# A decoder step on one Trainium2 core: the last 16 prompt queries as two leading chunks of the sample pipeline, and prompt output rows turned behind the next scores

## The chip, the cores and the metric

The program runs on one NeuronCore of a Trainium2 chip. The core has a matrix engine (PE, with its weight loads shown as PEld), a vector engine (DVE), a scalar engine (ACT), a general engine (POOL), and SP, which here only issues DMAs. The metric is the device time in microseconds of one execution; lower is better. PE works on operands in SBUF and writes to PSUM; DVE and ACT move results from PSUM to SBUF. The engines run their own instruction lists and wait for each other on semaphores.

## The reference

One inference step over 1024 prompt tokens (with 16 learned tokens ahead of them, so 1040 rows) and 8 sample tokens, each of which has a paged past of 4096 tokens. A first layer is a gated linear recurrence, the second is latent attention: all heads share a latent key/value row of 256 numbers and a rotary key of 64.

```python
def mla_scores(q_lat, q_rope, ckv, krope):
    s = jnp.einsum('bqhr,bkr->bhqk', q_lat, ckv) + jnp.einsum('bqhp,bkp->bhqk', q_rope, krope)
    return s.astype(jnp.float32) * ATTN_SCALE
...
    s = jnp.where((k_pos[None, :] <= q_pos[:, None])[None, None], s, MASK_VALUE)
    p = jax.nn.softmax(s, axis=-1).astype(ckv.dtype)
    return jnp.einsum('bhqk,bkr->bqhr', p, ckv)
```

The sample tokens do the same over `cache_ckv[page_table]` and `cache_krope[page_table]` (4096 rows each) and their own new row. After attention come an output projection, a squared-ReLU MLP and a final norm.

## The kernel before, in words

All 1048 tokens are held as columns of one array `h` (1050 wide). The stages run one after the other, each a block of instruction lists for the five engines with a barrier between blocks: load, recurrence, projection, MLP, `latents`, `query_latent`, `prompt_attention`, `sample_attention`, projection, MLP, `finish`. Two of them matter here.

**`prompt_attention`** covers prompt queries 0 to 1023: 8 heads times 8 tiles of 128 queries are 64 units, in an order written out by hand (`ORDER_ROWS`). For each unit s PE turns the probabilities of s (`turn_probs`, L1647, transposes into the two banks of `M`), computes the scores of s + 2 (`scores`, L1635 and L1638), does pieces of projection work for the next head (`piece`, L185), and multiplies by the values of s (`values`, L1665). After every fourth unit the four finished rows of output tiles are turned as well (`turn_out_rows`, L1655), in a bank of `M` that the turned probabilities also use. ACT copies turned probabilities out of `M` (L1731), copies the turned output rows (L1740) and does the exponentials (L1721); it also splits rotary queries (L1714).

**`sample_attention`** handles the rest: the 16 last prompt queries (the "tail": 8 heads times 16 queries fill 128 rows) and the 8 sample tokens. First PE turns the key projection (L2084) and forms the latent queries (L2099). Then, before, the tail is done by itself: the 1040 prompt keys, read back from the output by SP (L2015, L2016), are turned (L2090, L2092, L2105), copied, scored in four blocks of 260 (L2113, L2114), the row maxima, exponentials and turned probabilities follow (L2272, L2053, L2126), and the values (L2132). In the same place the sample tokens' scores with each other's new rows are formed (`cross`, L2119, L2120). Only then the pipeline over the paged past starts: for each of 8 tokens two chunks of 16 key tiles. A chunk is four spans of four tiles: `turn(u)` transposes the keys of a span (L2145) and for every second span the rotary keys (L2153), ACT copies even spans (L2033), DVE odd ones (L2295) and the rotary keys (L2301). One turn of the loop for chunk n is: first turn of chunk n + 1, values of n - 1 (L2185), scores of n (L2165, L2170), three more turns, turned probabilities of n (L2177). The four spans' scores stand in four groups of 32 rows. POOL gathers the pages (L2007, L2008) into a ring of four; the ring's last slot holds the prompt keys until the tail is done. A closing part (L2212 to L2235) joins the chunks and applies the value projection `w_uv`.

The 16 chunk loops, the queue order on SP and POOL and the order on each engine are all written out in the code; no scheduler moves anything.

Of the kernel before, what the change touches and what calls it, by code (L numbers as in the profile page):

```python
# [6 lines left out]
F32 = mybir.dt.float32  # L7
# [65 lines left out]
def setup(nc, ctx, dram):  # L73
# [11 lines left out]
    k.w_raw = sb("w_raw", [P, 2, WB])  # L85
    k.w_hi = sb("w_hi", [P, 2, WB], F32R)
    k.w_lo = sb("w_lo", [P, 2, WB], F32R)
    k.rstd = sb("rstd", [P, T])
# [31 lines left out]
    k.ckv_one = sb("ckv_one", [P, KC, DEC])  # L120
    k.kr_one = sb("kr_one", [ROPE, DEC])
# [1057 lines left out]
def latents(k, keys):  # L1179
# [5 lines left out]
    with ExitStack() as mem:  # L1185
# [13 lines left out]
        with nc.Block() as block:  # L1199
# [83 lines left out]
            def _(dve):  # L1283
# [24 lines left out]
                nc.vector.tensor_copy(k.kr_one[:, :], kr32[:, PROMPT:NTOK]).then_inc(k.g_free, 1)  # L1308
# [9 lines left out]
                link(nc.vector.tensor_copy(k.ckv_one[:, :, :], c32[:, :, PROMPT:NTOK]))  # L1318
# [126 lines left out]
def prompt_attention(k, keys, scratch):  # L1445
# [52 lines left out]
    with ExitStack() as mem:  # L1498
# [42 lines left out]
        with nc.Block() as block:  # L1541
# [45 lines left out]
            def _(pe):  # L1587
# [309 lines left out]
PAIR_COLS = SPAN * P  # L1897


def sample_attention(k, scratch):  # L1900

    nc, dr = k.nc, k.dram
    every = DEC * CHUNKS
    with ExitStack() as mem:
        def sb(name, shape, dt=F32):
# [6 lines left out]
        uk_turned = sb("uk_turned", [P, HEADS * KC, P])  # L1914
        w_kv = k.w_raw[:, :, :].rearrange("p a n -> p (a n)").rearrange("p (t h n) -> p t h n", t=KC, n=P)
        q_all = k.rstd[:, 0:DEC * (KC + 2) * LANE].rearrange("p (b t n) -> p b t n", b=DEC, n=LANE)
# [13 lines left out]
        o_lat = uk_turned[:, :, :].rearrange("p a n -> p (a n)")[:, 0:KC * HEADS * ONE].rearrange(  # L1930
            "p (t h n) -> p t h n", t=KC, n=ONE)
        o_one = sb("o_one", [P, HEADS, T - SEQ])

        c_rows = pages[:, RING - 1, 0:NT * KV].rearrange("p (t n) -> p t n", n=KV)
        kr_rows = ropes[:, RING - 1, 0:NT * ROPE].rearrange("p (t n) -> p t n", n=ROPE)
        keys_out = o_all[:, :, :].rearrange("p a n -> p (a n)")
        c_turned = keys_out[:, 0:KC * PROMPT].rearrange("p (t n) -> p t n", n=PROMPT)
        kr_turned = keys_out[0:ROPE, KC * PROMPT:(KC + 1) * PROMPT]
        tail_prob = pages[:, RING - 1, NT * KV:NT * KV + PROMPT]
# [38 lines left out]
        def tile_of(n, j):  # L1978
            return pages[:, n % RING, j * KV:(j + 1) * KV]
# [14 lines left out]
        with nc.Block() as block:  # L1994
            @block.gpsimd
            def _(pool):
# [526 lines left out]
```

## Time and profile before

| | |
|---|---|
| median of 3 runs | 3271.95 us (3263.16 to 3274.47) |
| profiled execution, its own time | 3266.1 us |
| its span in the trace | 3264.3 us |
| PE busy | 2927.2 us, 90% of the span |
| mean granted clock of PE | 0.942 of full speed |
| start of the sample stage's first instruction on PE | 2102.49 us |

The span runs from the first to the last instruction of the profiled execution; the stages follow each other in it. Positions in the trace (such as 2102.49) are microseconds from its start. A wait is shown with what ended it, as `[13.79 <-DMA late<-in_causal]`. The granted clock is 1.00 at 2.4 GHz and 0.50 at 1.2 GHz.

### The profile page before, as it was taken

The numbers are of one execution on the slowest core, as the hardware profiler recorded it, in microseconds if no ns is written. First come the engines' busy times: TensorE is split into PE (matmuls) and PEld (weight loads), VectorE is DVE, ScalarE is ACT, GpSimd is POOL, SyncE is SP. The second block draws the span as 40 slices with busy tenths as digits, with TensorE's granted clock in tenths as the row PEclk, the third lists the DMA queues.
The fourth block names the chain that finished last, engine by engine and source line by source line (L and its number), as shares of the span: only waits on it lengthen the run. The fifth ranks groups of instructions, "written<-read, shape, count | busy, mean of one in ns | idle before, by whom it ended". The sixth has DMA issues, their size and how long they took to land. (4 is left out here: it accounts for less than half of the span.)

```text
span 3264.3 us, 51288 instructions
## 1 busy us (share of the span) xinstructions
PE 2927.2 (90%) x21729; PEld 2772.6 (85%) x21729; DVE 1371.4 (42%) x1689; ACT 527.5 (16%) x810; POOL 785.3 (24%) x455
## 2 busy tenths in 40 slices
PE   6999899749899999999866889699788999999998
PEld 6888888749899999999755888566588999999997
DVE  6466666641633333222545555334315333222333
ACT  3222222120200000000222333323102000000001
POOL 2112211012333333333211100001033333333331
PEclk9999999859999999999878999879799999999999
DMA  3111111020111111111110000246221111111112
GB/s 100 47 46 46 48 56 46 21 93 26 52 46 46 45 46 46 46 46 46 37 30 25 26 28 32 100 161 265 77 62 39 46 46 46 46 46 46 46 46 72
DMA packets 213553, 185.32 MB, mean 57 GB/s; under 512 B 22720, under 2 KB 201200, under 8 KB 211344
## 3 DMA queue, kind: packets, MB, share of 16 engines
q1 hardware_dynamic: 174544, 116.19, 11.8%
q0 software_dynamic: 4608, 41.95, 3.3%
q10 hardware_dynamic: 34240, 24.75, 2.5%
q8 instruction: 136, 2.23, 0.3%
q14 instruction: 25, 0.20, 0.0%
HBM read 163.97 MB, written 18.89 MB: 56 GB/s over the span
## 5 line engine op out<-in xcount | busy, mean ns | idle before, releaser
L157 POOL CAST w_hi<-w_raw 128x1024 fp32r<-128x1024 f32 (+3 forms) x206 | 210.1, 1020 | 2165.3 <-PEq L960 1530.7
L185 PE MATMUL G<-xg_lo_a,w_hi 128*128 128x350 f32 (+1 forms) x1980 | 464.3, 338 | 115.8 <-POOL w_lo L159 58.8
L159 POOL TENSOR_TENSOR w_lo<-w_raw,w_hi 128x1024 fp32r<-128x1024 f32 (+3 forms) x206 | 541.9, 2630 | 16.5
L185 PEld LDWEIGHTS G<-xg_lo_a,w_hi 128*128 128x128 f32 (+1 forms) x1980 | 343.2, 194 | 135.1 <-issue 61.9
L185 PE MATMUL G<-xg_hi_a,w_lo 128*128 128x350 f32 (+1 forms) x1980 | 449.8, 330 | 0.0
L185 PE MATMUL G<-xg_hi_a,w_hi 128*128 128x350 f32 (+1 forms) x1980 | 448.6, 330 | 0.0
L1123 DVE TENSOR_TENSOR h<-h,G 128x1050 f32<-128x1050 f32 x128 | 159.7, 1248 | 520.6 <-PE G L185 520.6
L185 PEld LDWEIGHTS G<-xg_hi_a,w_hi 128*128 128x128 f32 (+1 forms) x1980 | 350.4, 194 | 0.6
L185 PEld LDWEIGHTS G<-xg_hi_a,w_lo 128*128 128x128 f32 (+1 forms) x1980 | 348.7, 194 | 0.6
L185 PE MATMUL G<-a_hi,w_hi 128*128 128x350 f32 x1536 | 332.1, 324 | 0.0
L185 PE MATMUL G<-a_lo,w_hi 128*128 128x350 f32 x1536 | 332.1, 324 | 0.0
L185 PE MATMUL G<-a_hi,w_lo 128*128 128x350 f32 x1536 | 329.8, 322 | 0.0
L1065 ACT ACTIVATE a_hi<-ua 128x1050 fp32r<-128x1050 f32 x64 | 69.4, 1085 | 1222.4 <-DVE ua L1113 1222.4
L185 PEld LDWEIGHTS G<-a_lo,w_hi 128*128 128x128 f32 x1536 | 263.4, 189 | 0.0
L185 PEld LDWEIGHTS G<-a_hi,w_hi 128*128 128x128 f32 x1536 | 261.6, 189 | 0.0
L185 PEld LDWEIGHTS G<-a_hi,w_lo 128*128 128x128 f32 x1536 | 261.5, 189 | 0.0
L1110 DVE TENSOR_TENSOR ua<-G,rstd 128x1050 f32<-128x1050 f32 x64 | 80.1, 1252 | 403.8 <-PE G L185 403.7
L185 PE MATMUL G<-xg_lo_b,w_hi 128*128 128x350 f32 x960 | 209.2, 326 | 39.8 <-POOL w_lo L159 34.6
L185 PE MATMUL G<-xg_hi_b,w_lo 128*128 128x350 f32 x960 | 208.8, 326 | 0.0
L185 PE MATMUL G<-xg_hi_b,w_hi 128*128 128x350 f32 x960 | 208.2, 325 | 0.0
L185 PEld LDWEIGHTS G<-xg_lo_b,w_hi 128*128 128x128 f32 x960 | 164.6, 191 | 42.4 <-POOL w_lo L159 35.0
L1116 DVE TENSOR_TENSOR a_lo<-ua,a_hi 128x1050 fp32r<-128x1050 f32 x64 | 140.2, 2191 | 73.7 <-ACT a_hi L1065 73.7
(349 smaller groups left out, 3386.9 us busy)
## 6 DMA issues: line engine op xcount, KB each, us to landing
w_raw<-in_w_up SPq DMA_DIRECT2D x64, 512.0 KB, 4.1
w_raw<-in_w_down SPq DMA_DIRECT2D x64, 512.0 KB, 3.4
o_scratch<-o_head SPq DMA_DIRECT2D x8, 525.0 KB, 5.3
o_in<-o_scratch ACTq DMA_DIRECT2D x4, 1050.0 KB, 9.3
o_in<-a_scratch ACTq DMA_DIRECT2D x4, 1050.0 KB, 9.2
w_raw<-in_hg_wq SPq DMA_DIRECT2D x8, 512.0 KB, 4.3
w_raw<-in_hg_wf SPq DMA_DIRECT2D x8, 512.0 KB, 4.2
w_raw<-in_hg_wi SPq DMA_DIRECT2D x8, 512.0 KB, 4.2
```

Source lines behind the costliest of these rows:

```text
L157: nc.gpsimd.tensor_copy(high, raw).then_inc(k.w_hi_done, 1)
L159: nc.gpsimd.tensor_tensor(low, raw, high, ALU.subtract).then_inc(k.w_split, 1)
L185: last = nc.tensor.matmul(out, w(a, t), x(b, t, c), start=(t == 0 and (a, b) == ORDER[0]), stop=(t == nk - 1 and (a, b) == ORDER[-1]))
L1065: nc.scalar.activation(a_hi[:, half, j, :], a, ACT.Copy).then_inc(a_hi_there, 1)
L1110: nc.vector.tensor_tensor(in3(u), tile(k, (g0 + 1 + j) % 2), in3(k.rstd[:, :]), ALU.mult).then_inc(k.g_free, 1)
L1116: nc.vector.tensor_tensor(a_lo[:, half, j, :], a, a_hi[:, half, j, :], ALU.subtract).then_inc(a_ready, 1)
L1123: nc.vector.tensor_tensor(h, h, tile(k, (g0 + 1 + t) % 2), ALU.add).then_inc(k.g_free, 1)
```

## The change

Two edits. The first is in `prompt_attention`: `turn_out_rows` stands behind `scores(s + 2)` instead of ahead of it, at the 15 units where it occurs inside the loop.

The second is in `sample_attention`. The separate computation for the tail is gone. Its first 1024 keys become two chunks at the head of the pipeline (`EARLY` = 2, of one span each instead of four, with all 128 rows of the tail in place of four groups of 32), so there are 18 steps and spans 0 and 1 belong to the tail. The tail's last 16 keys (its own) are scored beside `cross` and have a softmax part of their own; the three parts are joined on DVE during later chunk loops (`tail_rests`, `tail_join`) with one exponential on ACT. `late`, the mask for the own keys, no longer belongs to what `rows_in` counts. POOL waits for the prompt rows before the first gather. `w_uv` has a buffer of its own and is loaded by SP behind the prompt rows, not by ACT. `uk_turned`, `tail_q` and others live in the space of `w_hi` and `w_lo`, and `ckv_one` and `kr_one` hold 24 columns instead of 8.

```diff
                     turn_probs(s)
+                    if s + 2 < UNITS:
+                        scores(s + 2)
                     if s % 4 == 0 and s:
                         turn_out_rows(s // 4 - 1)
-                    if s + 2 < UNITS:
-                        scores(s + 2)
...
+EARLY = SEQ // (SPAN * P)
+def spans_of(n):
+    return [n] if n < EARLY else [EARLY + (n - EARLY) * GROUPS_1 + j for j in range(GROUPS_1)]
+def chunk_of(u):
+    return u if u < EARLY else EARLY + (u - EARLY) // GROUPS_1
...
             def _(pool):
                 nc.gpsimd.memset(q_all, 0.0).then_inc(cleared, 1)
+                nc.gpsimd.memset(tail_qr, 0.0).then_inc(cleared, 1)
...
+                pool.wait_ge(rows_in, 64)
                 for n in range(every):
                     if n == RING - 1:
+                        pool.wait_ge(valued, EARLY)
                         pool.wait_ge(tail_valued, 1)
                     if n >= RING:
-                        pool.wait_ge(valued, n - RING + 1)
+                        pool.wait_ge(valued, EARLY + n - RING + 1)
...
             def _(sp):
+                for h in range(HEADS):
+                    sp.dma_start(late[h * TAIL:(h + 1) * TAIL, :], dr["causal"][0:TAIL, 0:TAIL]).then_inc(late_in, 16)
                 sp.dma_start(own[:, :], dr["ckv_sample"][:, 0, :]).then_inc(own_in, 16)
-                for h in range(HEADS):
-                    sp.dma_start(late[h * TAIL:(h + 1) * TAIL, :], dr["causal"][0:TAIL, 0:TAIL]).then_inc(rows_in, 16)
+                sp.wait_ge(rows_in, 64)
+                sp.dma_start(w_uv[:, :, :, :], dr["w_uv"].rearrange("(t p) h n -> p t h n", p=P)).then_inc(uv_in, 16)
...
+                pe.wait_ge(rows_in, 64)
+                turn(0)
+                pe.wait_ge(ql_out, KC + 2)
+                pe.wait_ge(tail_q_out, 3)
...
+                turn(1)
+                scores(0)
+                pe.wait_ge(own_out, 2)
+                pe.wait_ge(tail_exped, 1)
+                pe.transpose(T_BANK[0:TAIL, 0:P], tail_prob, k.ident[:, :]).then_inc(tail_pt_done, 1)
+                pe.wait_ge(tail_pt_out, 1)
+                nc.tensor.matmul(O[:, 1, :], tail_pt, c_rows[0:TAIL, FULL, :], start=True, stop=True).then_inc(tail_valued, 1)
+                turn_probs(0)
+                for n in range(1, steps):
+                    later = spans_of(n + 1) if n + 1 < steps else []
+                    if n == EARLY - 1:
                         values(n - 1)
+                        scores(n)
+                        for u in later:
+                            turn(u)
+                    else:
+                        for u in later[:1]:
+                            turn(u)
+                        values(n - 1)
+                        scores(n)
+                        if n == EARLY + 3:
+                            pe.wait_ge(tail_summed, 1)
...
+                def tail_join():
+                    dve.wait_ge(tail_weighed, 1)
+                    link(nc.vector.tensor_tensor(tail_sums[:, :], tail_sums[:, :], tail_weight[:, :], ALU.mult))
+                    link(nc.vector.reduce_sum(tail_stat[:, 2:3], tail_sums[:, :], AX.X))
+                    link(nc.vector.reciprocal(tail_stat[:, 3:4], tail_stat[:, 2:3]))
+                    link(nc.vector.tensor_scalar(tail_weight[:, :], tail_weight[:, :], tail_stat[:, 3:4], None, ALU.mult))
+                    link(nc.vector.tensor_scalar(o_tail[:, 0, :], o_tail[:, 0, :], tail_weight[:, 0:1], None, ALU.mult))
+                    for a in range(1, parts):
+                        link(nc.vector.scalar_tensor_tensor(out=o_tail[:, 0, :], in0=o_tail[:, a, :],
+                                                            scalar=tail_weight[:, a:a + 1], in1=o_tail[:, 0, :],
+                                                            op0=ALU.mult, op1=ALU.add))
+                    dve.sem_inc(tail_summed, 1)
```

PE in `prompt_attention`, unit 28, before: the turned probabilities (L1647), the output rows (L1655), then the scores of unit 30 (L1635, L1638).

```order
L1647 MATMUL M<-ident,prob 128x128 x3
L1655 MATMUL M<-ident,a_o_rows 128x128 [waits a_turn_out,a_o_there]
L1655 MATMUL M<-ident,a_o_rows 128x128 x3
L1635 MATMUL G<-xg_lo_a,xg_hi_a 128x512 [waits a_exp]
L1635 MATMUL G<-xg_hi_a,xg_lo_a 128x512
```

The same place in the changed kernel, whose line numbers are 3 higher here: the end of the scores of unit 30, the output rows, and the first product of the next piece (L188).

```order
L1638 MATMUL G<-xg_hi_a 128x384
L1641 MATMUL G<-kr_lo,xg_lo_a 128x384
L1641 MATMUL G<-kr_hi,xg_lo_a 128x384
L1658 MATMUL M<-ident,a_o_rows 128x128 [waits a_turn_out,a_o_there]
L1658 MATMUL M<-ident,a_o_rows 128x128 x3
L188 MATMUL G<-xg_lo_a,w_hi 128x350 [waits a_piece_out]
```

The four transposes and their wait stand behind ten score products instead of ahead of them.

PE at the head of the sample stage, before: from the latent queries (L2099) to the tail's values (L2132), twelve of its rows in their order.

```order
L2099 MATMUL M<-q_one,uk_turned 128x24 x15
L2105 MATMUL G<-ident,pages 128x128 x16
L2113 MATMUL G<-o_all,one_pt 128x260 [waits s_tail_out,s_tail_q_out]
L2113 MATMUL G<-o_all,one_pt 128x260
L2114 MATMUL G<-o_all,one_pt 128x260
...
L2119 MATMUL M<-rstd,ckv_one 8x64 [waits s_ql_out]
L2119 MATMUL M<-rstd,ckv_one 8x64
L2120 MATMUL M<-rstd,kr_one 8x64
L2126 MATMUL G<-ident,pages 128x128 [waits s_tail_exp]
L2126 MATMUL G<-ident,pages 128x128 x7
L2126 MATMUL M<-ident,pages 16x128
L2132 MATMUL M<-pages,keys_turned 128x256 [waits s_own_out,s_tail_pt_out]
```

The changed kernel from the same queries (L2115) to the scores of the second early chunk (L2154; `spare_lo` holds the tail's queries and its own keys' probabilities).

```order
L2115 MATMUL M<-q_one,spare_hi 128x24 x15
L2130 MATMUL G<-ident,pages 128x128 [waits s_rows_in]
L2130 MATMUL G<-ident,pages 128x128 x7
...
L2190 MATMUL M<-ckv_one,spare_lo 128x16 x2
L2191 MATMUL M<-kr_one,spare_lo 128x16
L2130 MATMUL G<-ident,pages 128x128 x8
L2154 MATMUL M<-keys_turned,spare_lo 128x512 [waits s_pair_out,s_span_out0]
L2154 MATMUL M<-keys_turned,spare_lo 128x512
L2160 MATMUL M<-ropes_turned,spare_lo 128x2x128 x2
L2197 MATMUL M<-ident,spare_lo 16x128 [waits s_tail_exped,s_own_out]
L2199 MATMUL G<-pages,spare_lo 128x256 [waits s_tail_pt_out]
L2167 MATMUL M<-ident,one_prob 128x128 [waits s_pt_out,s_exped]
```

The queries no longer stand behind the wait for the rows, and the tail's keys are turned, scored and used with the pipeline's instructions.

DVE in chunk step 4 of the changed kernel: the maxima (L2295, L2296), the join of the tail's parts (L2328 to L2334), and only then the copy of the next odd span (L2284), which before stood right behind the maxima.

```order
L2296 TENSOR_SCALAR one_bottom<-one_tops 128x1 [waits dve_chain]
L2328 TENSOR_TENSOR tail_sums<-tail_sums,tail_weight 128x3 [waits s_tail_weighed]
L2329 TENSOR_REDUCE tail_stat<-tail_sums 128x1 [waits dve_chain]
L2330 RECIPROCAL tail_stat<-tail_stat 128x1 [waits dve_chain]
L2331 TENSOR_SCALAR tail_weight<-tail_weight,tail_stat 128x3 [waits dve_chain]
L2332 TENSOR_SCALAR spare_lo<-spare_lo,tail_weight 128x256 [waits dve_chain]
L2334 SCALAR_TENSOR_TENSOR spare_lo<-spare_lo,tail_weight 128x256 [waits dve_chain] x2
L2284 COPY keys_turned<-G 128x1024 [waits dve_chain,s_scored,s_span_done]
```

Seven instructions stand between the maxima and the copy in that step; two stand there in step 3, one in step 5.

## Rows read from the trace of the kernel before

**Rows 1.** The page: engine busy time, then the granted PE clock in 40 slices.
```profile
PE 2927.2 (90%) x21729; PEld 2772.6 (85%) x21729; DVE 1371.4 (42%) x1689; ACT 527.5 (16%) x810; POOL 785.3 (24%) x455
...
PEclk9999999859999999999878999879799999999999
```

**Rows 2.** Windows: stretch, its length, busy PE, PEld, DVE, ACT, POOL, clock, DMA.
```profile
1790.00:2080.00 290.00, 258.96 (x1682) 232.97 (x1680) 153.90 (x388) 108.68 (x242) 22.70 (x32) 0.98 0.08 26
2102.00:2165.00 63.00, 43.16 (x174) 32.94 (x175) 10.90 (x32) 6.82 (x8) 8.71 (x10) 0.58 0.47 180
2165.00:2323.00 158.00, 151.86 (x1694) 104.44 (x1692) 77.29 (x111) 51.41 (x78) 22.47 (x24) 0.99 0.55 211
```

**Rows 3.** Timeline, sample stage: start, length, engine, line, instruction, idle before.
```profile
2102.49 3.65 PE L2084 MATMUL G<-ident,w_raw 128*128 128x128 f32 x16 [3.22 <-PEq L1541]
...
2106.17 1.22 DVE L2251 COPY uk_turned<-G 128x1024 f32<-128x1024 f32 x1 [2.13 <-PE G L2084]
...
2119.93 1.92 PE L2090 MATMUL G<-ident,ropes 128*64 128x128 f32 x8 [13.79 <-DMA late<-in_causal]
...
2122.15 7.02 PE L2099 MATMUL M<-q_one,uk_turned 128*128 128x24 f32 x32
...
2128.99 3.20 PE L2105 MATMUL G<-ident,pages 128*128 128x128 f32 x16
...
2152.84 7.32 PE L2132 MATMUL M<-pages,keys_turned 128*128 128x256 f32 x18 [1.04 <-DVE keys_turned L2283]
```

**Rows 4.** Timeline, PE in the chunk loops.
```profile
2173.03 1.04 PE L2145 MATMUL G<-ident,pages 128*128 128x128 f32 x8
...
2182.89 1.04 PE L2145 MATMUL G<-ident,pages 128*128 128x128 f32 x8
...
2184.30 1.93 PE L2185 MATMUL G<-pages,one_pt 128*32 128x256 f32 x32
2186.05 1.90 PE L2165 MATMUL M<-keys_turned,rstd 128*32 128x512 f32 x16
...
2188.74 1.97 PE L2145 MATMUL G<-ident,pages 128*128 128x128 f32 x16
...
2191.38 1.09 PE L2145 MATMUL G<-ident,pages 128*128 128x128 f32 x8 [0.24 <-DVE keys_turned L2295]
```

**Rows 5.** DMA view, 2102:2108: queue, packets, MB, share; then 2100:2325, landing us.
```profile
q1 hardware_dynamic: 1947, 1.29, 73.3%
...
pages<-in_cache_ckv,page_rows POOLq DMA_INDIRECT x16, 8.3
```

**Rows 6.** Timeline, DVE and ACT instructions of a chunk.
```profile
2169.38 0.69 DVE L2306 TENSOR_REDUCE one_tops<-M 128x1 f32<-128x512 f32 x1 [2.17 <-PE M L2170]
2170.11 0.15 DVE L2307 TENSOR_SCALAR one_bottom<-one_tops 128x1 f32<-128x1 f32 x1
...
2173.23 0.60 ACT L2046 ACTIVATE one_pt<-M 128x512 f32<-128x512 f32 x1 [0.95 <-PE M L2177]
```

**Rows 7.** Windows: clock under thin work, at the stage's end, and in it.
```profile
2330.00:2352.00 22.00, 21.48 (x98) 21.12 (x98) 0.39 (x2) 0.00 (x0) 0.00 (x0) 0.50 0.00 1
...
2132.00:2135.00 3.00, 0.89 (x5) 0.67 (x4) 1.23 (x1) 1.93 (x2) 0.00 (x0) 1.00 0.00 0
2135.00:2136.00 1.00, 1.00 (x3) 0.38 (x3) 0.00 (x0) 0.00 (x0) 0.00 (x0) 0.50 0.00 0
```

**Rows 8.** PE's waits, 1700:2100: total us, times, longest; then timeline of one place.
```profile
PE M L1655 <- ACT a_pt L1731: 12.4, 8, 3.0
...
1922.71 1.08 ACT L1714 ACTIVATE xg_hi_a<-a_qr 64x1050 fp32r<-64x1050 f32 x1 [2.59 <-DVEq L1830]
...
1924.42 0.63 PE L1655 MATMUL M<-ident,a_o_rows 128*128 128x128 f32 x4 [3.00 <-ACT a_pt L1731]
1924.80 0.47 PE L1635 MATMUL G<-xg_lo_a,xg_hi_a 128*128 128x512 f32 x1
...
1926.92 0.32 PE L185 MATMUL G<-xg_lo_a,w_hi 128*128 128x350 f32 x1
```

More of the change, by code:

```diff
@@ L1905, in sample_attention @@
     every = DEC * CHUNKS
+    steps = EARLY + every
     with ExitStack() as mem:
@@ L2163, in scores @@
                     for t in range(KC):
-                        for j in range(GROUPS_1):
-                            nc.tensor.matmul(S[group(j), :].rearrange("p (a n) -> p a n", n=P), q_all[:, b, t, :],
-                                             now(n, j)[:, :, t, :], start=(t == 0), stop=False)
+                        for j, u in enumerate(spans_of(n)):
+                            rows, q = (group(j), q_all[:, b, t, :]) if n >= EARLY else (slice(0, P), tail_q[:, t, :])
+                            nc.tensor.matmul(S[rows, :].rearrange("p (a n) -> p a n", n=P), q, now(u)[:, :, t, :],
+                                             start=(t == 0), stop=False)
@@ L2206, in _ @@
                     turn_probs(n)
-                values(every - 1)
+                values(steps - 1)
                 for c in range(CHUNKS):
@@ L2219, in _ @@
                 pe.wait_ge(w_out, 1)
-                pe.wait_ge(o_out, every)
+                pe.wait_ge(o_out, steps + 1)
                 pe.wait_ge(own_in, 16)
@@ L2314, in _ @@
                 pair_copy(0)
+                own_part()
                 span_copy(1)
[L2316 to L2332 removed]
@@ L2333, in _ @@
-                values_out(every - 1)
+                maxima(0)
+                dve.wait_ge(tail_pt_done, 1)
+                nc.vector.tensor_copy(tail_pt, T_BANK[0:TAIL, 0:P]).then_inc(tail_pt_out, 1)
+                dve.wait_ge(tail_valued, 1)
+                nc.vector.tensor_copy(o_tail[:, EARLY, :], O[:, 1, :]).then_inc(o_out, 1)
+                own_scores()
+                for n in range(1, steps):
+                    later = spans_of(n + 1) if n + 1 < steps else []
+                    if n == EARLY - 1:
+                        values_out(n - 1)
+                        maxima(n)
+                    for u in later[:1]:
+                        pair_copy(u // 2)
+                    if n != EARLY - 1:
+                        values_out(n - 1)
+                        maxima(n)
+                    if n == EARLY + 1:
+                        tail_rests()
+                    if n == EARLY + 2:
+                        tail_join()
+                    if n == EARLY + 3:
+                        dve.wait_ge(tail_lat, 1)
+                        nc.vector.tensor_copy(o_lat[:, :, :, 0:TAIL], T_BANK[:, 0:KC * P].rearrange(
+                            "p (t h n) -> p t h n", t=KC, n=TAIL)).then_inc(lat_out, 1)
+                    for u in later[1:]:
+                        if u % 2:
+                            span_copy(u)
+                        else:
+                            pair_copy(u // 2)
```

298 lines of the change are left out of this document (123 added, 175 removed).

## The prediction, made before the run

> **What bounds the kernel now.** I read the page first: PE is busy for 90% of the span, no other engine above 42% [rows 1]. The kernel is a chain of stages, each fed by PE, so a change is worth what it takes off PE's own time line: work, waits, or a lower clock. Then the windows by stage. In the prompt attention PE is busy 259 of 290 us at a clock of 0.98; in the first 63 us of the sample stage it is busy 43 at a clock of 0.58; in the 158 us of chunk loops 152 at 0.99 [rows 2]. So the loops have almost nothing left, and the head of the sample stage is where waits and half-speed work stand. Third, the timeline of that head [rows 3]: after the turned key projection PE stands 13.8 us for a DMA, the mask `late`, and everything behind it, the latent queries too, comes later although the queries need no rows. Then follow the queries (7.0 us), the tail's own pass with its hand-offs, and its values, which end at 2160.1; the first full loop (first turn of chunk 2) begins at 2173.03 [rows 4]. Last, PE's waits in the prompt attention: the largest one that the change touches is that of the output rows for ACT's copy, 12.4 us in 8 places [rows 8].
>
> **The sample stage, step by step.** I rebuild PE's list for the changed order, in the times of the trace of before. The head stays at the lower clock, as it is there now.
> - The copies of the turned key projection end at 2107.4 (DVE: 2106.17 + 1.22 [rows 3]). ACT's goes no later, since its DMA issue is gone. The queries start there, not at 2122.15, and take 7.0: 2114.4.
> - `turn(0)`: 8 + 4 transposes at 0.20 each (3.20 for 16 [rows 3]) = 2.4: 2116.8. Their rows must be there. By 2108 the queue q1 had moved 1.29 MB [rows 5], and the four row transfers are 1.33 MB in all (1040 rows of 320 numbers), so they are in at about 2109: 5 us or more to spare.
> - Six small products (the sample tokens' own and the tail's own keys) at the 0.44 of a query product (7.02 for 16) = 2.6: 2119.4. `turn(1)`, 8 transposes, 1.6: 2121.0.
> - `scores(0)`: a chunk's scores take 2.7 at full clock (2186.05 to 2188.74 [rows 4]); there four row groups run abreast, here one takes all 128 rows, so the time is the same. At half clock 5.4: 2126.4.
> - The maxima 0.69 + 0.15 [rows 6], DVE's small copy 0.3 and the hand-offs: 2127.6. One value product 0.8 (7.32 for nine [rows 3]), turned probabilities 0.8, ACT's copy 0.6 [rows 6] and a hand-off: 2129.9.
> - `values(0)` 1.75 (2184.30 to 2186.05) and `scores(1)` 2.7 at full clock: 2134.4. Four turns and the turned probabilities are what is left of a loop of 9.86 (2173.03 to 2182.89 [rows 4]), 9.86 - 1.75 - 2.69 = 5.4: 2139.8. Chunk 0's loop, which now has the values of `values(1)` in it, 9.86: 2149.7.
>
> At this point before stands at 2173.03, so the head gives 23.3 us. Back goes the join. PE waits for DVE's span copy in the loop already (0.24 [rows 4]), so what stands ahead of that copy is paid. Step 3: two small operations at 0.19 (0.15 and a gap of 0.04 [rows 6]), 0.4. Step 4: four small ones, 0.8, and three over 256 columns. Their bounds are the 0.15 of one column and the 0.69 of 512 [rows 6]; I take 0.37 each, 1.1. Step 5: two transposes and a 256-wide copy, 0.4. Together 2.7; the bounds are nothing (all of it in DVE's idle time, over half of the stage [rows 2]) and 4. The head and the join: 20.6.
>
> What I cost at nothing: the mask's eight DMAs, now outside `rows_in`. Their cover is the time until PE has the own scores (2119.4), and beyond, since `scores(0)` doesn't wait for them and the own part needs only to end before 2126.4; if they land 10 us later, the excess is paid. The gathers, which now wait for the rows: they start at about 2109 instead of 2103.6, the first page is needed at 2134.4. The 16 gathers landed in 8.3 us at the median [rows 5]; the first three are queued together with `w_uv`. At 384 GB/s (211 at a share of 0.55 in the loops [rows 2]) 2.6 MB a page and 1 MB of `w_uv` put the first in by about 2120, the second by 2127, the third by 2134; the second and third are needed at 2139.8 and 2149.7. If that cover were gone, each us late is a us of the sum. SP's list: the mask stands ahead of `own`, and `w_uv` behind the wait for the rows; both are used some 200 us later. POOL's extra memset (a quarter of the first) is over before DVE needs it. The own scores' diagonal moves on DVE to a place where DVE waits for PE anyway.
>
> **The clock.** It is the unknown of the head. It rose only when wide work had run without a gap: it is 0.50 through 22 us of thin products with all of PE busy [rows 7]. After rising in the present head it stood at 1.00 while PE had 0.89 us of work in 3 us, and was 0.50 in the next us [rows 7]. In the new order transposes and 512-wide scores run from 2119.4 to 2126.4, so the rise can come inside `scores(0)` (up to 2.5 us less) or at its end; the stretch from 2126.4 to 2129.9 is as thin as the one that lost it (then `values(0)` and part of `scores(1)` go at half speed, up to 4.4 more). I take these two against each other: 0.
>
> The Trainium skill, TensorE: Matmul & The Clock Gate (Part 1, the HAM clock gate), says that throttling is the default and activity releases it. Taken as it stands, PE busy from 2107.4 on would be released within the queries. The trace doesn't agree for thin products, as the 22 us show.
>
> **The prompt attention.** The wait is ended by ACT's copy of turned probabilities; behind it stand the scores of s + 2, which need none of it. They now go first. In three of the eight places the wait is 3.0, and the scores that go ahead take 2.1 there (1924.80 to 1926.92 [rows 8]), so 0.9 stays; in the other five it is shorter than 2.1 and vanishes. 12.4 - 3 x 0.9 = 9.7. ACT copies the output rows later by the scores' time, ahead of its next exponential, but that needs those scores and DVE's maxima, so it is no later; the other seven places had no wait and have none. Bounds: nothing (ACT's chain sets the pace) and 12.4. The values of s, queued behind, come nearer to the copy they need; I take 9.0.
>
> **The sum.** 20.6 + 9.0 = 29.6. Against the profiled execution's own 3266.1 that is 3236.5; it lies 6 below the median of the runs, 3271.95, from which it would be 3242. I say 3240.
>
> **Rivals.**
> - ScalarE keeps the pace of the prompt attention. For: the three long waits end behind its split of rotary queries, which stands ahead of the copy [rows 8]. Against: PE is busy 89% there, ACT 37% [rows 2]. The second term is 0: 3249. Chance 0.12.
> - The clock falls in the thin stretch and stays down until the pages' turns are done (2139.8): some 9 us of PE work doubled. For: rows 7. Against: the work behind it is dense, like the loops at 0.99. 3249. Chance 0.10.
> - The clock is up from the queries on. Half of 7.0 + 2.4 + 2.6 + 1.6 + 5.4 is 9.5 less: 3231. Against it the 22 us of rows 7. This is what the page's rule would give. Chance 0.04.
> - The hand-offs of the two early chunks, which nothing hides, cost twice what I gave them, and the join its upper bound: 7 less gained, 3247. Chance 0.08.
> - The slower one: gathers reach the end of their cover. A gather is issued when a ring slot is free, nearly two loops (about 17 us) before its use. If they land later than that now, with the ring shifted by two steps, PE waits in each of 13 loops; at 2.3 us a loop (19.3 us to landing) the whole gain is eaten, at 20.5 it is 3283. Against: the median of 8.3, and the distance in loops is unchanged. Chance 0.03.
> - My forecast, 0.63.
>
> **Range.** Alone the forecast reaches from 3230 (full clock in part of the head, all 12.4) to 3250. The two rivals at 3249 and the one at 3247 are inside the upper end, and I leave a few us for the runs' own spread of 11: 3228 to 3254. A measurement of this kernel tells changes from about 0.3%, 9.8 us. Faster by more: all but the last rival and some of the worst mixtures, 0.94. Within: 0.03. Slower: 0.03.
>
> **What would show it.** The query products start within 6 us of the stage's first instruction, with no wait for a DMA ahead of them; the first full-width turn of a second paged chunk comes 47 us after the stage's start, not 70.5; no PE wait on a gather; the loops stay at 9.9 but for three, together 2.7 longer; PE's waits at the output rows fall from 12.4 to about 3. Wrong would be: a DMA wait at `turn(0)` or `turn(2)`; the clock at 0.50 beyond 2135; the waits at the output rows turning up at `values` or at `turn_probs` instead; loops longer than 9.9 throughout.

## The result and the profile after

| | before | after |
|---|---|---|
| median | 3270.11 us (3263.16 to 3274.47, 4 runs) | 3227.23 us (3224.74 to 3229.64, 4 runs) |
| ratio, 95% interval | | 0.9871 [0.9851, 0.9891] |
| profiled execution, its span | 3264.3 us | 3224.6 us |
| first prompt exponential on ACT, at | 1765.2 | 1762.4 |
| from there to the sample stage's first PE instruction | 337.3 us | 326.6 us |
| the sample stage: from there to the start of the last product that weighs the chunks' values (L2228, in after L2244) | 241.6 us | 217.2 us |
| behind that, to the end of the span | 920.2 us | 918.4 us |

The gain is 42.9 us (1.3%). The profiled pair differs by 39.7 us: 24.4 in the sample stage, 10.7 in the prompt attention, and 4.6 in parts whose code is the same, 2.8 ahead of the two stages and 1.8 behind them. The page of after, the same two lines as in [rows 1]:

```profile
PE 2911.5 (90%) x21720; PEld 2763.0 (86%) x21720; DVE 1376.1 (43%) x1700; ACT 528.8 (16%) x815; POOL 786.8 (24%) x456
...
PEclk8999999959999999999887999999699999999999
```

PE's busy time fell by 15.7 us with only nine instructions fewer. They are not the same instructions (the tail's scores are 512 columns wide, not 260), so how much of the 15.7 is the clock isn't separated here. The other 24 us are time in which PE stood.

**The head.** The timeline of after, PE alone. It answers to [rows 3]; the stage's first PE instruction is at 2088.98.

```profile
2093.22 7.02 PE L2115 MATMUL M<-q_one,spare_hi 128*128 128x24 f32 x32 [1.32 <-DVE spare_hi L2270]
2100.07 1.95 PE L2130 MATMUL G<-ident,pages 128*128 128x128 f32 x8
...
2105.36 1.88 PE L2154 MATMUL M<-keys_turned,spare_lo 128*128 128x512 f32 x4
2107.08 1.03 PE L2160 MATMUL M<-ropes_turned,spare_lo 128*128 128x256 f32 x4
2107.94 0.27 PE L2197 MATMUL M<-ident,spare_lo 128*16 128x128 f32 x1
2109.27 0.69 PE L2199 MATMUL G<-pages,spare_lo 16*128 16x256 f32 x2 [1.05 <-DVE spare_lo L2344]
2109.89 0.66 PE L2167 MATMUL M<-ident,one_prob 128*128 128x128 f32 x4
2111.24 1.99 PE L2176 MATMUL G<-pages,one_pt 128*128 128x256 f32 x8 [0.69 <-ACT one_pt L2070]
...
2120.68 1.04 PE L2130 MATMUL G<-ident,pages 128*128 128x128 f32 x8
...
2130.41 1.04 PE L2130 MATMUL G<-ident,pages 128*128 128x128 f32 x8
```

No wait for a DMA is left. The queries start 4.2 us after the stage's start, `turn(0)` 11.1, `scores(0)` 16.4, `values(0)` 22.3, and the first turn of the second paged chunk 41.4 (before: 70.5). `scores(0)` takes 2.6 us (2105.36 to 2107.94), not 5.4. The windows say why. First after, with its thin stretch as last row, then before at its own rise; the clock is the column behind POOL, as in [rows 7].

```profile
2094.00:2097.00 3.00, 3.00 (x16) 3.00 (x15) 0.00 (x0) 0.00 (x0) 0.54 (x1) 0.50 0.38 64
...
2100.00:2103.00 3.00, 3.00 (x17) 2.67 (x17) 0.78 (x4) 0.94 (x1) 2.08 (x4) 0.50 1.16 490
2103.00:2104.00 1.00, 1.00 (x10) 0.66 (x8) 0.60 (x1) 0.08 (x1) 0.78 (x1) 0.79 0.69 295
2104.00:2106.00 2.00, 2.00 (x14) 1.69 (x14) 0.97 (x5) 0.32 (x2) 0.00 (x0) 1.00 0.94 403
...
2108.00:2111.00 3.00, 1.50 (x8) 0.71 (x6) 1.83 (x6) 1.19 (x3) 0.00 (x0) 1.00 1.01 433
```

```profile
2129.00:2131.00 2.00, 2.00 (x11) 2.00 (x12) 0.69 (x3) 0.00 (x0) 0.00 (x0) 0.50 0.35 139
2131.00:2132.00 1.00, 1.00 (x8) 0.95 (x6) 0.00 (x0) 0.00 (x0) 0.00 (x0) 0.71 0.01 4
```

In after the clock goes from 1.2 to 2.4 GHz between 2103 and 2104, right after the transposes that began at 2100.07 and beside the first small products, and it stays up through the thin stretch. In before it rose between 2131 and 2132, during the transposes that had begun at 2128.99 [rows 3]. Ahead of both rises PE had done transposes without a pause; neither came within the query products. That the transposes are enough for it isn't shown by this: the section on e9 has two traces in which they were not.

**The join.** From one chunk's values to the next's (L2176) steps 2 to 5 last 9.82, 10.16, 13.80 and 10.18, and the next ones 9.86 us, so it costs 4.6 us. The timeline of after in the long step, DVE and PE:

```profile
2147.70 0.15 DVE L2296 TENSOR_SCALAR one_bottom<-one_tops 128x1 f32<-128x1 f32 x1
2147.77 0.15 DVE L2328 TENSOR_TENSOR tail_sums<-tail_sums,tail_weight 128x3 f32<-128x3 f32 x1
...
2149.00 1.00 DVE L2334 SCALAR_TENSOR_TENSOR spare_lo<-spare_lo,tail_weight 128x256 f32<-128x256 f32 x2
2150.22 1.22 DVE L2284 COPY keys_turned<-G 128x1024 f32<-128x1024 f32 x1 [0.21 <-DVE spare_lo L2334]
...
2151.50 1.97 PE L2130 MATMUL G<-ident,pages 128*128 128x128 f32 x8 [2.68 <-DVE keys_turned L2284]
```

PE stands 2.68 us, and then the clock is down, as the windows of after show:

```profile
2152.00:2153.00 1.00, 1.00 (x6) 1.00 (x5) 0.04 (x1) 0.00 (x0) 0.00 (x0) 0.50 0.71 291
2153.00:2154.00 1.00, 1.00 (x7) 1.00 (x6) 0.49 (x1) 0.00 (x0) 0.00 (x0) 0.50 0.00 0
2154.00:2156.00 2.00, 2.00 (x18) 1.76 (x20) 0.85 (x2) 1.16 (x2) 0.00 (x0) 0.85 0.00 0
```

**The prompt attention.** PE's waits of after from 1700 to 2100, against the 12.4 of [rows 8]:

```profile
PE M L1658 <- ACT a_pt L1734: 2.9, 3, 1.0
```

PE's other waits of this stretch are as before within 0.4 us.

**The transfers.** The DMA view of after, 2089 to 2320; the last number is us from issue to landing:

```profile
pages<-out_ckv_prompt SPq DMA_DIRECT2D x1, 1024.0 KB, 5.5
...
pages<-in_cache_ckv,page_rows POOLq DMA_INDIRECT x16, 8.2
```

### The profile page after: what moved, and what is told of

It reads as the page before. It is cut to its first block and busy times, and to the rows that moved or that the text cites. A ratio compares the mean times of both kernels' runs of the same rounds, so it can differ in the third digit from the quotient of the medians.

```text
span 3224.6 us, 51306 instructions
## 1 busy us (share of the span) xinstructions
PE 2911.5 (90%) x21720; PEld 2763.0 (86%) x21720; DVE 1376.1 (43%) x1700; ACT 528.8 (16%) x815; POOL 786.8 (24%) x456
## 5 line engine op out<-in xcount | busy, mean ns | idle before, releaser
L188 PE MATMUL G<-xg_lo_a,w_hi 128*128 128x350 f32 (+1 forms) x1980 | 466.0, 338 | 115.2 <-POOL w_lo L162 58.9
L188 PEld LDWEIGHTS G<-xg_lo_a,w_hi 128*128 128x128 f32 (+1 forms) x1980 | 343.2, 194 | 135.2 <-issue 61.0
L188 PE MATMUL G<-xg_hi_a,w_lo 128*128 128x350 f32 (+1 forms) x1980 | 448.3, 329 | 0.0
L188 PE MATMUL G<-xg_hi_a,w_hi 128*128 128x350 f32 (+1 forms) x1980 | 447.4, 329 | 0.0
L188 PEld LDWEIGHTS G<-xg_hi_a,w_lo 128*128 128x128 f32 (+1 forms) x1980 | 348.5, 194 | 0.6
L188 PEld LDWEIGHTS G<-xg_hi_a,w_hi 128*128 128x128 f32 (+1 forms) x1980 | 348.2, 193 | 0.6
L188 PE MATMUL G<-a_lo,w_hi 128*128 128x350 f32 x1536 | 330.2, 323 | 0.0
L188 PE MATMUL G<-a_hi,w_lo 128*128 128x350 f32 x1536 | 329.8, 323 | 0.0
L188 PE MATMUL G<-a_hi,w_hi 128*128 128x350 f32 x1536 | 329.4, 322 | 0.0
L188 PEld LDWEIGHTS G<-a_lo,w_hi 128*128 128x128 f32 x1536 | 262.4, 189 | 0.0
L188 PEld LDWEIGHTS G<-a_hi,w_hi 128*128 128x128 f32 x1536 | 261.1, 188 | 0.0
L188 PEld LDWEIGHTS G<-a_hi,w_lo 128*128 128x128 f32 x1536 | 260.6, 189 | 0.0
L188 PE MATMUL G<-xg_lo_b,w_hi 128*128 128x350 f32 x960 | 210.2, 327 | 40.1 <-POOL w_lo L162 34.9
L188 PE MATMUL G<-xg_hi_b,w_hi 128*128 128x350 f32 x960 | 208.0, 325 | 0.0
L188 PE MATMUL G<-xg_hi_b,w_lo 128*128 128x350 f32 x960 | 208.0, 325 | 0.0
L188 PEld LDWEIGHTS G<-xg_lo_b,w_hi 128*128 128x128 f32 x960 | 165.2, 191 | 42.7 <-POOL w_lo L162 35.3
```

Source lines behind the costliest of these rows:

```text
L188: last = nc.tensor.matmul(out, w(a, t), x(b, t, c), start=(t == 0 and (a, b) == ORDER[0]), stop=(t == nk - 1 and (a, b) == ORDER[-1]))
```

## The experiments

Medians of before in the three series, as run beside them: 3267.63 (e1 to e4), 3265.58 (e5 to e8), 3268.02 (e9 to e12).

### The two edits apart, and after again: e1, e2, e3

e1 is before with the first edit alone:

```diff
-                    if s % 4 == 0 and s:
-                        turn_out_rows(s // 4 - 1)
                     if s + 2 < UNITS:
                         scores(s + 2)
+                    if s % 4 == 0 and s:
+                        turn_out_rows(s // 4 - 1)
```

> The kernel before with the first edit alone (output rows turned behind the scores of s + 2). Theory: the wait at the output rows is taken off PE's list, 12.4 us less what the scores don't cover; the changed kernel has 2.9 us of it left and its sample stage starts 13.5 us earlier, 2.3 us of that from before the prompt attention. So this kernel is 9.5 to 11.2 us faster than before, and its wait for ACT's copy at the output rows is 2.9 us in all. Rival 1, ACT's chain sets the pace: under 3 us faster, with the waits back at the values. Rival 2, the gain of the pair is more than the sum of its parts (through the clock at the head of the sample stage): 6 us or less here. Ahead of the prompt attention nothing is changed, so its first exponential stays at 1765 us if the 2.3 us came with the changed kernel's layout, and moves by some us either way from run to run if they are chance.

e2 is after with this edit undone, so the sample stage alone is changed.

> The changed kernel with the first edit undone (output rows ahead of the scores again). Theory: the edits are independent, the stage of the samples gives its 24 us (234.8 us from its first instruction to the first copy of the next stage, against 258.9), so 24 to 28 us faster than before, and with the first experiment the two add up to the whole, 40 to 43. Rival: the sample stage's early full clock (it rose 14.5 us after the stage's start) is luck of where the stage starts in time, and another start gives it some us later: then the stage takes up to 240 us and the gain is 19 to 22.

e3 is the changed kernel, run in the same series as a base for e4.

> The changed kernel again, beside the others on the same chip, as a yardstick. 40 to 44 us faster than before. If the 4.4 us that the first two profiles differ outside the two changed stages (2.3 ahead, 2.1 behind) belong to the change, this profile shows them again within 0.5; if they are chance, they differ by a us or more from it.

Measured: e1 3251.92 (-15.7, ratio 0.9948 [0.9935, 0.9962]), e2 3241.83 (-25.8, 0.9920 [0.9907, 0.9934]), e3 3225.60 (-42.0, 0.9870 [0.9855, 0.9885]). The two alone give 41.5 together, so they add up. In e1's trace the prompt attention is 11.0 us shorter and the wait 2.9, in 3 places, the same as in after; in e2's it is 12.4, in 8 places, and the stage as long as in before (337.1). So the wait's size is shown: 9.5 us. The gain of e1 lies above the 9.5 to 11.2 that I had expected: its median gained 4.7 more than its prompt attention did. In the profiles 1.9 of it stands ahead of the stage, in code that is the same; where the rest comes from is open.

### The join's place: e4, e11

DVE's two parts of the join stand behind that step's copies of turned keys, and ACT's exponential one step later.

```diff
-                    if n == EARLY + 1:
-                        tail_rests()
-                    if n == EARLY + 2:
-                        tail_join()
...
                         else:
                             pair_copy(u // 2)
+                    if n == EARLY + 1:
+                        tail_rests()
+                    if n == EARLY + 2:
+                        tail_join()
```

> The changed kernel with the join of the tail's three parts moved on DVE from behind the maxima to the end of its chunk step, behind the span copies, and with the exponential of the weights one step later on ACT. Theory: step 4 of the changed kernel takes 13.8 us against 9.86, 2.4 of it DVE's seven operations ahead of the span copy and 1.5 the half clock after PE's 2.7 us stand; at the end of the step DVE has over 4 us of idle time before it is waited for. So steps 3 and 4 go back to 9.9 and the kernel is 4.2 us faster than the changed one. Rival: the join delays the next step's rotary copy and values instead, and 2 us or more stay. The clock is 1.00 in steps 3 to 5 by the theory.

Measured: 3223.88, 1.7 below e3 (0.9864 [0.9849, 0.9879]). The trace answers where the median doesn't: the sample stage is 213.0 us, 4.1 shorter than e3's, with steps of 9.86, 9.88 and 10.18, and the clock is 1.00 through them. The timeline of e4, where the join now stands in the long step's place:

```profile
2149.12 1.09 PE L2130 MATMUL G<-ident,pages 128*128 128x128 f32 x8 [0.26 <-DVE keys_turned L2284]
...
2151.41 0.16 DVE L2328 TENSOR_TENSOR tail_sums<-tail_sums,tail_weight 128x3 f32<-128x3 f32 x1
...
2152.65 1.01 DVE L2334 SCALAR_TENSOR_TENSOR spare_lo<-spare_lo,tail_weight 128x256 f32<-128x256 f32 x2
```

PE waits 0.26 instead of 2.68. The profiled executions of e4 and e3 differ by only 0.4 all the same, because code that the edit doesn't touch took longer in e4: 3.0 us ahead of the prompt attention (first exponential at 1764.9, in e3 at 1762.0) and 1.4 behind the sample stage. Whether the same holds for the medians one profile each can't tell. So the same kernel ran again, beside after again (e12, below):

> The kernel with the join moved, once more, as the yardstick of the last one and against the changed kernel of the same call. In its first timing its sample stage was 4.1 us shorter than the changed kernel's but its median only 1.7 lower. Theory: 4 us lower than the changed kernel in truth, the rest was chance ahead of the stage (its first exponential of the prompt attention came at 1764.9 against 1762.0, in unchanged code), so 3 to 5 us lower here or within 2 us of that. Rival: something behind the stage gives the 4 us back each time, and it is 1 to 2 us lower again.

Measured: 3223.03, 4.5 below e12's 3227.50. The sample stage is 213.2 against 217.3. The median now moves by what the stage does.

### Does the stand itself lower the clock: e8

The changed kernel with 20 transposes more, on PE, in the place where it stands. Their results go to a bank that nobody reads.

```diff
+                            if n == EARLY + 2 and u == later[3]:
+                                for x in range(20):
+                                    pe.transpose(T_BANK[:, x % 4 * P:(x % 4 + 1) * P], k.ident[:, :], k.ident[:, :])
                             turn(u)
```

> The changed kernel with 20 transposes of the identity into a free bank ahead of the last turn of chunk step 4, where PE stood 2.7 us for DVE's join. They are work added only to keep PE busy and change nothing else. Theory: the clock fell to 0.50 for 3.4 us because PE stood; filled, it stays at 1.00, the step takes 12.3 to 12.6 us instead of 13.8, although more work is in it. Rival: the clock doesn't depend on that stand (it fell by chance or by the rate of work before), the added work comes on top and the step takes 13.8 or more.

Measured, one run: 3221.50. The timeline and a window of e8:

```profile
2145.80 2.35 PE L2221 MATMUL M<-ident 128*128 128x128 f32 x20
2148.65 1.09 PE L2130 MATMUL G<-ident,pages 128*128 128x128 f32 x8 [0.50 <-DVE keys_turned L2287]
```

```profile
2148.00:2152.00 4.00, 3.50 (x38) 3.01 (x40) 2.89 (x4) 1.51 (x2) 0.00 (x0) 1.00 0.42 172
```

PE can start its next turn no earlier, since DVE is late as before, and yet the step takes 12.30 us, not 13.80. Work that is of no use saves 1.5 us, by the clock alone. So the long step's excess of 3.9 is 2.4 of standing and 1.5 of half clock.

### What the old wait hid: e5

Before, with the mask on a semaphore of its own, on which only DVE's masking waits.

```diff
-                    sp.dma_start(late[h * TAIL:(h + 1) * TAIL, :], dr["causal"][0:TAIL, 0:TAIL]).then_inc(rows_in, 16)
+                    sp.dma_start(late[h * TAIL:(h + 1) * TAIL, :], dr["causal"][0:TAIL, 0:TAIL]).then_inc(late_in, 16)
...
-                pe.wait_ge(rows_in, (4 + HEADS) * 16)
+                pe.wait_ge(rows_in, 4 * 16)
...
                 dve.wait_ge(tail_scored, 1)
+                dve.wait_ge(late_in, HEADS * 16)
```

> The kernel before with one change: the mask's eight DMAs have a semaphore of their own, which only DVE's add of the mask waits for; the tail's own pass stays as it was. Theory: of the 24 us of the sample stage about half is nothing but the wait for the mask. The rows were in by 2108 to 2109 in the trace of before and PE went on at 2119.9, so the stage's first part starts some 11 us earlier and the kernel is 9 to 11 us faster; the rest of the 24 is the tail's pass inside the pipeline. Rival: the rows themselves come late when the gathers are issued beside them; then PE still waits at their first transpose, now for the rows, and under 4 us are gained. Second rival: the first gathered page is then the one waited for, when the pipeline starts at about 2149.

Measured: 3256.98 over 10 runs (-8.6, 0.9974 [0.9963, 0.9985], just under the 9 to 11 expected); the sample stage is 10.6 us shorter. In this profile the prompt attention, whose code is that of before, lasts 342.3 us against 337.3, at a mean clock of 0.96 against 0.98. The timeline of e5, whose stage starts at 2108.30:

```profile
2116.58 1.92 PE L2090 MATMUL G<-ident,ropes 128*64 128x128 f32 x8 [4.64 <-DMA ropes<-out_krope_prompt]
```

The wait falls from 13.79 to 4.64. Of the 24.4 us of the sample stage, 10.6 are to be had with this line alone. The other 13.8 must be the rest of the wait, the separate pass, and the clock, less the join; no run takes them apart.

### Transfers in the new order: e6, e7

e6 takes POOL's wait for the rows away, so the gathers start 6 us earlier and share the engines with the rows. e7 is e6, and PE waits for the mask ahead of `turn(0)`.

```diff
-                pool.wait_ge(rows_in, 64)
...
                 pe.wait_ge(rows_in, 64)
+                pe.wait_ge(late_in, HEADS * 16)
                 turn(0)
```

> The changed kernel without POOL's wait for the prompt rows ahead of the first gather. Theory: that wait hides completely. The rows were in 7.2 us after the stage's start, PE asked for them after 11.1, and no wait on a page is seen. Here the gathers start 6 us earlier, the mask lands later (16 to 17 us after the stage's start, as before the change) and the rows at 7 to 8 us; the time from the stage's first PE instruction to the last of the closing products stays at 217.2 us, within 1. Rival: the gathers slow the rows or the mask so that PE or DVE waits, at turn(0) or at the own part, 2 us or more.

> As the last one, and PE waits for the mask too ahead of turn(0): the wait of the kernel before put back into the changed one. Theory: the mask lands 17 us after the stage's start, PE would ask for it at 11.1, so PE waits 6 us there; the clock, which rises in the transposes and products behind the queries, rises later or needs its time again, so the stage gets 6 to 9 us longer, 223 to 226 us. Rival: in the changed order the mask's transfers are no longer behind the gathers' (they are issued earlier) and the wait is under 2 us.

Measured, one run each: e6 3226.96, with a sample stage of 217.4 (after 217.2) and no wait for the rows: POOL's wait is free, and so is its absence. e7 3228.64, with a stage of 220.9. The timeline of e7, whose stage starts at 2087.45:

```profile
2102.66 1.94 PE L2129 MATMUL G<-ident,pages 128*128 128x128 f32 x8 [4.22 <-DMA late<-in_causal]
```

The mask lands some 15 us after the stage's start: eight transfers of 1 KB, behind the rows and, in e7, beside gathers that start early. The wait of 4.2 costs 3.5 against e6, less than the 6 to 9 I had written. The mask was in after 15.2 us, not 17, and the clock rose all the same: between 2105 and 2106 (0.71 in that window), some 3 us after `turn(0)` began, as in after.

### The order of queries and `turn(0)`: e9

The changed kernel with `turn(0)` ahead of the query products instead of behind them.

```diff
                 pe.wait_ge(uk_out, 2)
+                pe.wait_ge(rows_in, 64)
+                turn(0)
                 for h in range(HEADS):
...
                 ins.then_inc(ql_done, 1)
...
-                pe.wait_ge(rows_in, 64)
-                turn(0)
```

> The changed kernel with turn(0) ahead of the query products instead of behind them. The prompt rows were in 7.2 us after the stage's start and turn(0) could begin at 4.2, so 3 us of wait come back. Theory on the clock: it rises in the dense transposes that follow the queries (3.4 us after they begin, in the changed kernel), so that the own products, turn(1) and scores(0) run at full clock; with the thin query products between turn(0) and the rest, the rise comes only in scores(0). Then from the stage's first PE instruction to values(0) it takes 22.2 + 3.0 + 3 to 5 = 28 to 30 us. Rival: the clock rises a fixed time after PE began to work and the order doesn't matter: 25 to 25.5 us.

Measured, one run: 3234.81. The timeline of e9 (stage's start 2089.97), and its windows:

```profile
2096.92 1.94 PE L2123 MATMUL G<-ident,pages 128*128 128x128 f32 x8 [4.05 <-DMA ropes<-out_krope_prompt]
...
2099.51 6.86 PE L2179 MATMUL M<-q_one,spare_hi 128*128 128x24 f32 x32
...
2109.48 1.97 PE L2123 MATMUL G<-ident,pages 128*128 128x128 f32 x8
2111.24 3.58 PE L2147 MATMUL M<-keys_turned,spare_lo 128*128 128x512 f32 x4
```

```profile
2112.00:2114.00 2.00, 2.00 (x4) 0.86 (x3) 0.71 (x1) 0.00 (x0) 0.00 (x0) 0.50 1.10 455
2114.00:2116.00 2.00, 1.80 (x7) 0.81 (x5) 0.27 (x1) 0.00 (x0) 0.00 (x0) 0.83 1.07 455
```

`values(0)` comes 28.8 us after the stage's start (22.3 in after). 4.05 is the wait for the rows, which the queries had covered; set against after's own wait of 1.32 ahead of the queries it costs 2.7. The rest is mostly half clock: `turn(1)` takes 1.76 to the next instruction (0.93 in after) and `scores(0)` 4.3 (2.6). PE was busy, but for one stand of 0.78 us, through 6.9 us of queries and the small products, and the clock stayed at 0.50 till `turn(1)` and `scores(0)` ran. The instructions are those of after. In the nine profiles that have after's head (after, e2, e3, e4, e6, e8, e10, e11, e12) the clock rose between 14 and 16 us after the stage's start, in e7, with a stand of 4.2 us put ahead of `turn(0)`, after 18, and in e9 after nearly 25. So the order decides when it rises, and a stand ahead of `turn(0)` doesn't keep it down; e9 itself is one profile. How much of the work that follows `turn(0)` in after is needed for the rise wasn't tried.

Nor is it shown that a row of transposes is enough. The old head has 16 of them (L2105) behind the same queries in before, in e1 and in e5. In before the clock rose while they ran. In e1 (3.65 us from 2116.11) and in e5 it didn't, and it stayed at 0.50 through the tail's score products behind them, 260 columns wide and without a pause. The timeline and two windows of e5:

```profile
2125.65 3.65 PE L2105 MATMUL G<-ident,pages 128*128 128x128 f32 x16
```

```profile
2126.00:2129.00 3.00, 3.00 (x16) 2.90 (x14) 0.55 (x3) 0.00 (x0) 0.00 (x0) 0.50 0.96 400
2132.00:2144.00 12.00, 12.00 (x24) 6.17 (x22) 0.00 (x0) 0.00 (x0) 0.00 (x0) 0.50 0.29 119
```

Before, too, goes through these score products at 0.50, PE being busy in 11.00 of 11.00 us from 2136 to 2147. So the rise on which the head of after depends came in all ten profiles that have `turn(0)` behind the queries, while the rise in before, on the old order, came in one profile of three. Which instructions bring it stays open.

### Both leftovers removed: e10, with e12 as its base

e10 is e4 and, in the prompt attention, ACT's split of rotary queries held until after the next copy of turned probabilities, the copy for which PE still waited 1.0 us in three places.

```diff
                     copy_turned(s)
+                    for at in held:
+                        split_high(at)
+                    held = []
...
                         if x[0] == "turn" and x[2] == NB - 1:
-                            split_high(2 * x[1])
+                            held.append(2 * x[1])
```

> The kernel with the join moved (the fourth experiment), and in the prompt attention ACT's split of the rotary queries stands behind the copy of the next turned probabilities instead of ahead of it. In the changed kernel 2.9 us of the wait at the output rows are left, in the three places with that split. Theory: they vanish, and the prompt attention is 2.5 to 3 us shorter than in the kernel with the join moved alone, 43 to 50 us faster than before in all. Rival: DVE, which waits for the split with its next maxima queued behind, passes the delay on, and the gain is under 1 us.

> The changed kernel once more beside these, 40 to 44 us faster than before.

Measured: e10 3220.45 (-47.6, 0.9851 [0.9834, 0.9867]), e12 3227.50 (-40.5, 0.9873 [0.9856, 0.9889]). e10 is 7.0 below after and 2.6 below e11. In its trace the output rows wait for ACT no more; PE's waits there, 1700 to 2100, are one row:

```profile
PE M L1658 <- DVE a_o_rows L1865: 0.5, 1, 0.5
```

Its prompt attention lasts 322.0 us and its sample stage 214.0, against 326.7 and 217.3 in e12. Not all of the 4.7 us is the edit: the prompt attention of the changed kernel itself lasts 324.3 to 326.7 in its profiles. Against e4's 324.5 e10 is 2.5 shorter, which is what was expected. It is the fastest of the versions here.

## Why the prediction was right and wrong

I said 3240, from 3228 to 3254; it came out at 3227.23, just below the range. What the two edits take away went as described: the DMA wait, the separate pass, the wait at the output rows. The account of the clock in the head was wrong. The sum was 29.6: the sample stage gave 3.8 more, the prompt attention 1.7 more, the unchanged parts of the profiled pair 4.6, and the medians lie 3.2 further apart than the profiled pair. That is the 42.9. So of the 13.3 that are missing 5.5 lie in the stages that I had reckoned, and 7.8 in what the forecast had no term for. The gain itself isn't luck: it was 42.0 beside e3 and 40.5 beside e12.

- **The step that failed is the clock.** I wrote that the head "stays at the lower clock", charged the small products, `turn(1)` and `scores(0)` at half, and set the remaining term to 0, because a rise inside `scores(0)` and a loss in the thin stretch would cancel. I let the stretch that could bring a rise begin at `turn(1)` and left `turn(0)` out of it. The clock rose in the small products right behind `turn(0)` and wasn't lost. The head's loop of the second paged chunk came 5.8 us sooner than forecast (41.4 for 47.2). Small products, `turn(1)` and `scores(0)` make 4.5 of it: 5.1 us (2102.80 to 2107.94) for 2.6 + 1.6 + 5.4. The key projection's turn makes 0.7, 2.92 for 3.65 [rows 3]: in after the stage began before the clock had gone down, in e2 it took the 3.65 again. The rest is small. `turn(0)` took 2.7 for 2.4, since the 3.20 of [rows 3] that I scaled has a piece at full clock in it. "It rose only when wide work had run without a gap" names what had run, and isn't enough for a rise: in e5 it stayed at 0.50 through 12 us of 260-wide products.
- **The join was sized 2.7 and is 4.6.** In step 4 I reckoned 1.9 us of standing over the 0.24 of a plain loop; it was 2.4. What I left out is what a stand does next: 1.5 us by the clock (e8). Steps 3 and 5 cost 0.3 each, against 0.4. e4 shows that nearly all of it needn't be paid.
- **The prompt attention.** The wait went from 12.4 to 2.9, against "12.4 - 3 x 0.9 = 9.7": as forecast, and the three places with 1.0 left are those where I had put 0.9. I took 9.0 for fear of later waits, which didn't come. The remaining 1.2 of the 10.7 us isn't explained, and it is less than what the same code shows. With the new order the stage lasts 326.3 to 326.7 us in five profiles (after, e1, e9, e11, e12) and 324.3 to 324.5 in five (e3, e4, e6, e7, e8); the first five have a clock of 0.91 from 1770 to 1790, the others 1.00. With the old order it is 337.3, 337.1 (e2) and 342.3 (e5). So this term is 9.5 by the wait, and 10.7 to 12.9 by the stage against before's one profile. Whether the edit itself makes the dips of the clock rarer is open.
- **What I cost at nothing cost nothing:** `w_uv`, the gathers (8.2 us to landing, e6), POOL's memset, the mask. Had `turn(0)` waited for the mask too, it would have cost about 3.5 (e7 against e6).
- **Rows of the prompt keys:** due 6.5 us after the stage's start, they came at 7.0 to 7.5 (PE's wait in e9, POOL's in after), and at 8.3 in e5, beside gathers: in time behind 7 us of queries, and 4 us too late without them.
- **The rivals.** ScalarE's pace: no, the wait vanished and the stage shortened. The clock down until the pages' turns: no, 1.00 from 2104 on. Up from the queries: no, 0.50 in them. Its 3231 lies nearer to the result than 3240 by luck: it gave the clock 9.5 us, the head came 5.8 sooner, and the rest of the distance is other terms. Hand-offs twice as long: no, 3.3 us from the end of `scores(0)` to `values(0)`, as reckoned. Gathers late: no (and 3.5 us in each of 13 loops make 45, so its upper figure should have been 3285, not 3283).
- **Outside the stages:** the first prompt exponential is at 1762.4 in after and 1765.2 in before, and at 1761.6 to 1766.6 in the other profiles, with after's own code at 1762.0, 1762.4 and 1766.6. So 2.8 us here are within what the same code shows, and so are 1.8 behind the stages (918.2 to 921.3 in all profiles). A range for this kernel has to hold them; mine left little room at its lower end. The medians have moved more than the stages elsewhere too, by 4.7 in e1 and 2.3 in e2, and less in e5 by 2.0; that part stays open.

The Trainium skill, TensorE: Matmul & The Clock Gate says in Part 1 (the HAM clock gate) that activity releases the throttle, and in Part 4 (PE-mode transpose) that full clock does not engage for transpose mode. By the first, the queries alone would have been enough. By the second, transposes would have kept the clock down. The traces disagree with the first: products of 24 columns left it at 0.50 with PE busy in 3.00 of 3.00 us, and so did 12 us of 260-wide ones in e5. They disagree with the second as a general rule for these fp32 transposes: it rose within L2105's in before (2131 to 2132), and 20 of them in a stand held it at 1.00 in e8, where the bare stand had brought it to 0.50. In e1 and e5 it stayed down through the same transposes.

## What to carry to other kernels

When two orders of the same instructions are free, put work that needs no transfer first, so that the wait is covered, and try which order has the clock up when the wide products come; here it was transposes between the thin products and the wide ones. One profile isn't enough for that: the old order had the early rise in one of three. A short chain on a side engine belongs behind the copy for which the main engine waits, and what it costs there is the main engine's stand plus the slow stretch after it. When you price a head that starts at half clock, look in the trace for what ran just before each rise and not only for what ran while the clock stayed down, and then look whether the same instructions ran elsewhere without a rise.

## What the runs showed of the hardware that I had not expected

- The clock rose during or right behind a run of 128 x 128 transposes (begun 2100.07, up in 2103 to 2104 in after; begun 2128.99, up in 2131 to 2132 in before), and not in 7 us of query products of 24 columns, with PE at 3.00 of 3.00 busy. The same 16 transposes as in before brought no rise in e1 and e5.
- It stayed at 0.50 through 12 us of score products 260 columns wide, with PE at 12.00 of 12.00 busy (2132 to 2144 in e5), and through 11 us of them in before.
- In after it stayed at 1.00 in a stretch with PE 1.50 of 3.00 busy (2108 to 2111), and went to 0.50 after one stand of 2.68 us between full-speed work (2152 to 2154).
- Twenty useless transposes in a stand made the kernel's step 1.5 us shorter (13.80 to 12.30).
- Eight transfers of 1 KB, issued right behind 1.3 MB, landed 15 us after the stage's start in e7 and 17 in before, the 1.3 MB after 7 (e9) to 8 (e5).
- One more short dip to half clock in the prompt attention (0.91 against 1.00 from 1770 to 1790) goes with a stage about 2.2 us longer (326.6 against 324.4) in the same code.
